# A projection computed with seven half products instead of eight, and its weight sums made partly by adding transfers

## The reference, cut to what matters

```
def swiglu(h, w_in, w_out):
    gu = h @ w_in
    gate, up = gu[..., :D_FF], gu[..., D_FF:]
    return (jax.nn.silu(gate) * up) @ w_out

        x = x + mla_attention(...)
        x = x + 0.5 * swiglu(rms_norm(x, g[2]), ffn_w_in[l, 1], ffn_w_out[l, 1])
return rms_norm(x, final_norm)
```

## Time and profile before

| what | value |
|---|---|
| time, median of 3 runs | 1777.91 us (1776.92 to 1777.92) |
| profiled execution, first to last instruction | 1777.1 us |
| PE busy | 1749.7 us (98%) |
| DVE / ACT / POOL busy | 931.8 / 651.0 / 322.9 us |
| traffic | 206.50 MB, mean 116 GB/s |

### The profile page before, as it was taken

One profiled execution on the slowest core, in us unless ns is written; L12 is line 12 of the kernel. 1 busy time (PEld: TensorE's weight loads), 2 busy tenths in 40 slices (PEclk: granted clock), 3 DMA queues, 4 the chain that ended last, 5 costly groups with the idle time before them and its releaser, 6 DMA issues.

```text
span 1777.1 us, 22440 instructions
## 1 busy us (share of the span) xinstructions
PE 1749.7 (98%) x8598; PEld 1432.7 (81%) x8598; DVE 931.8 (52%) x1066; ACT 651.0 (37%) x896; POOL 322.9 (18%) x276
## 2 busy tenths in 40 slices
PE   9999999997999999999999999999999999999998
PEld 6888887876888888888888888888777888888887
DVE  7778898648555334433374444333774544433333
ACT  6332333347334333322253333222574443333222
POOL 8997273015013000000100000000200200000000
PEclk9999999999999999999999999999999999999999
DMA  5464556698333333323323332333310333323321
GB/s 192 128 171 132 172 149 167 205 319 274 119 95 96 99 101 94 94 95 96 94 83 112 101 94 94 95 96 100 101 36 8 121 97 94 94 94 96 102 86 48
DMA packets 80788, 206.50 MB, mean 116 GB/s; under 512 B 24048, under 2 KB 34416, under 8 KB 79696
## 3 DMA queue, kind: packets, MB, share of 16 engines
q1 hardware_dynamic: 69664, 189.86, 34.2%
q0 software_dynamic: 2592, 13.51, 2.3%
q10 hardware_dynamic: 8464, 2.20, 0.5%
HBM read 182.46 MB, written 23.07 MB: 116 GB/s over the span
## 4 chain that ended last, share of the span: by engine, by line
PE 85%; DVE 6%; ACT 3%; DMA 2%; issue 2%; SPq 1%; ACTq 0%; DVEq 0%
PE bank L1642 27%; PE bank L1644 27%; PE bank L1643 27%; DVE w_split L1183 2%; PE bank L2002 1%; ACT w_split L766 1%; DMA op_slot<-s_ops 1%; DVE g_split L1197 1%; PE bank L1981 1%; DMA s_y<-u_and_y 1%; ACT x_gained L797 0%; ACTq L799 0%; DMA s_ops<-ops_out 0%; DMA x_res<-xT 0%; SPq L448 0%
## 5 line engine op out<-in xcount | busy, mean ns | idle before, releaser
L1183 DVE TENSOR_TENSOR w_split<-w_raw,w_split 128x1024 fp32r<-128x1024 f32 x296 | 404.2, 1370 | 607.3 <-ACT w_split L766 606.3
L1642 PE MATMUL bank<-h_split,w_split 128*128 128x512 f32 x1504 | 589.9, 392 | 5.7 <-DVE gate L1195 2.5
L1644 PE MATMUL bank<-h_split,w_split 128*128 128x512 f32 x1504 | 585.9, 390 | 0.0
L1643 PE MATMUL bank<-h_split,w_split 128*128 128x512 f32 x1504 | 585.9, 390 | 0.0
L766 ACT ACTIVATE w_split<-w_raw 128x1024 fp32r<-128x1024 f32 x296 | 311.9, 1058 | 606.3 <-PE bank L1644 598.0
L1642 PEld LDWEIGHTS bank<-h_split,w_split 128*128 128x128 f32 x1504 | 282.6, 188 | 69.3 <-DVE gate L1195 4.6
L1643 PEld LDWEIGHTS bank<-h_split,w_split 128*128 128x128 f32 x1504 | 282.8, 188 | 59.3 <-issue 1.2
L1644 PEld LDWEIGHTS bank<-h_split,w_split 128*128 128x128 f32 x1504 | 282.7, 188 | 59.2
L1642 PE MATMUL bank<-g_split,w_split 128*128 128x512 f32 (+1 forms) x854 | 328.3, 384 | 0.4 <-DVE g_split L1416 0.4
L1644 PE MATMUL bank<-g_split,w_split 128*128 128x512 f32 (+1 forms) x854 | 327.6, 384 | 0.0
L1643 PE MATMUL bank<-g_split,w_split 128*128 128x512 f32 (+1 forms) x854 | 327.6, 384 | 0.0
(11 more groups left out here) (298 smaller groups left out, 1148.0 us busy)
## 6 DMA issues: line engine op xcount, KB each, us to landing
w_raw<-wstream SPq DMA_DIRECT2D x296, 512.0 KB, 3.5
op_slot<-s_ops SPq DMA_DIRECT2D x5, 2048.0 KB, 12.0
s_ops<-ops_out SPq DMA_DIRECT2D x16, 512.0 KB, 3.1
op_slot<-s_ops POOLq DMA_DIRECT2D x3, 2048.0 KB, 14.1
s_ops<-c_pow POOLq DMA_DIRECT2D x8, 512.0 KB, 4.8
s_ops<-k_window SPq DMA_DIRECT2D x64, 64.0 KB, 3.4
x_res<-xT SPq DMA_DIRECT2D x8, 256.0 KB, 7.1
s_u<-x_gained ACTq DMA_DIRECT2D x8, 256.0 KB, 10.1
```

What stands on the lines that cost most here:

```text
L1183: tt(W[:, r, 1, :], RAW[:, r, :], W[:, r, 0, :].bitcast(F32), ALU.subtract).then_inc(s_lo, 1)
L1642: mm(bank, hi, x_hi, start=start, stop=True, skip_group_check=True)
L1643: mm(bank, hi, x_lo, start=False, stop=True, skip_group_check=True)
L1644: return mm(bank, lo, x_hi, start=False, stop=True, skip_group_check=True)
```

## The change

For the last feed-forward the 512 tokens are taken as two halves and the 8 input tiles as even and odd ones. A pair of a gate and an up tile is then a 2 x 2 block product, and it is computed with seven products of half the size and sums, in place of eight (pair 0 keeps the old form). A product is 4 blocks x 3 matmuls of 256 tokens: 84 matmuls a pair, for 21 pairs. The products need four sums of weight blocks (S1 to S4) and four sums of input tiles (T1 to T4). S1 and S3 are made by a transfer that GpSimd issues and that adds into the loaded block; S2 and S4 are made by GpSimd additions. DVE and ACT join the products in PSUM. The feed-forward is cut in two parts of 11 inner tiles: pairs 0 to 10, then all 8 output tiles over these, then pairs 11 to 21 and the output tiles again. Weights lie in 14 slots of 128 x 512 (in place of four packs of 1024), with loads, splits and products in a hand-written order. Some semaphores of earlier stages are merged; their waits stay where they were.

```diff
+SEVEN = {1: (A11, B11), 2: (A12, B21), 3: (S4, B22), 4: (A22, T4), 5: (S1, T1), 6: (S2, T2), 7: (S3, T3)}
+SLOTS = 14
+SPLITS = {1: (A12, 2), 2: (S1, 2), 3: (S4, 1), 4: (S3, 2)}
...
 SP
+            sp.wait_ge(s_used, WO + 5)
+            load_sum1(1)
...
+                    sp.wait_ge(s_prod, DONE[5, u - 2])
+                    load_sum1(u)
+                    sp.wait_ge(s_prod, DONE[2, u - 2])
+                    load_first(u)
+                    if u > first:
+                        sp.wait_ge(s_prod, DONE[4, u - 3])
+                        load_sum3(u - 1)
...
 GpSimd
+            def add_sum1(u):
+                pool.wait_ge(s_ld[unit_slot(u, S1)], LOADED[u, S1])
+                pool.dma_start(raw(u, S1), wunit[u - 1][:, 0:512], accum_op=ALU.add).then_inc(s_sum1, 16)
...
+            def sum2(u):
+                pool.wait_ge(s_ld[unit_slot(u, A12)], LOADED[u, A12])
+                pool.wait_ge(s_sum1, 16 * u)
+                tt(raw(u, S2), raw(u, S1), raw(u, A11), ALU.add).then_inc(s_sums, 1)
+            def sum4(u):
+                pool.wait_ge(s_sums, 2 * u - 1)
+                tt(raw(u, S4), raw(u, S2), raw(u, A12), ALU.add).then_inc(s_sums, 1)
+            def unit_sums(u):
+                add_sum1(u)
+                pool.wait_ge(s_prod, DONE[6, u - 2])
+                sum2(u)
+                pool.wait_ge(s_prod, DONE[3, u - 2])
+                sum4(u)
+            for k in range(1, 6):
+                square_sum(N_IN1B, k)
+            add_sum1(1)
+            sum2(1)
+            pool.wait_ge(s_used, WO + 6)
+            sum4(1)
...
+            for u in range(3, 11):
+                unit_sums(u)
+                add_sum3(u - 1)
...
 ACT
+            unit_hi(1, 2)
+            act.wait_ge(s_kv_read, DT - 1 + 4)
+            product_input(4)
+            product_input(5)
+            act.wait_ge(s_used, WO + DT)
+            product_input(6)
+            act.wait_ge(s_x, X_BASE[WO] + DT)
+            product_input(7)
...
+            for u in range(2, 10):
+                unit_hi(u + 1, 1)
+                copy_fifth(u)
+                copy_first(u)
+                silu(u - 1)
+                unit_hi(u + 1, 2)
+                unit_hi(u + 1, 3)
+                unit_hi(u, 4)
+                copy_first_and_sixth(u)
+                unit_g_hi(u - 1)
...
 DVE
+            slots_lo(1, 1)
+            slots_lo(1, 2)
+            product_lo(4)
+            product_lo(5)
+            add_wo(DT - 1)
+            product_lo(6)
+            product_lo(7)
+            t_sums(2)
+            t_sums(3)
+            slots_lo(1, 3)
+            t_lo(2)
+            t_lo(3)
+            mean_rcp(N_IN1B, BK[6])
+            slots_lo(2, 1)
+            slots_lo(2, 2)
+            gate_scale(0)
+            slots_lo(2, 3)
+            slots_lo(1, 4)
+            gate_up(0)
+            for u in range(2, 10):
+                gate_sum(u - 1)
+                unit_g_lo(u - 2)
+                gate_scale(u - 1)
+                slots_lo(u + 1, 1)
+                up_second(u - 1)
+                slots_lo(u + 1, 2)
+                slots_lo(u + 1, 3)
+                slots_lo(u, 4)
+                gate_up(u - 1)
...
 PE
+            def unit(u, first):
+                if u >= 3:
+                    pe.wait_ge(s_read, F_BASE[FFN1B] + u - 2)
+                unit_product(5, u)
+                unit_product(1, u)
+                if u > first:
+                    pe.wait_ge(s_snap, snap(u - 1, 2))
+                    unit_product(7, u - 1)
+                pe.wait_ge(s_snap, snap(u, 0))
+                unit_product(2, u)
+                pe.wait_ge(s_snap, snap(u, 1))
+                unit_product(6, u)
+                if u > first:
+                    pe.wait_ge(s_up, u - 1)
+                    unit_product(4, u - 1)
+                unit_product(3, u)
...
+            stat(N_IN1B, BK[6])
+            pe.wait_ge(s_t_lo, 4)
+            for u in range(1, 11):
+                unit(u, 1)
+            for d in range(DT):
+                out_tiles_of(0, d)
+            for u in range(11, 22):
+                if u in (11, 12):
+                    pe.wait_ge(s_x, X_AT[0] + (6 if u == 11 else 8))
+                unit(u, 11)
+            for d in range(DT - 1):
+                out_tiles_of(1, d)
...
-                    if q == 1 and f == 8:
+                    if q == 1 and f == 5:
                         half_stat(0)
-                    if q == 1 and f == 14:
+                    if q == 1 and f == 9:
                         half_rstd(0)
```

More of the change, by code:

```diff
@@ new lines, with unit_slot, products_of @@
+PAIR_SLOTS = (10, 12)
+H_PLACE = (2, 3, 0, 1)
+def unit_slot(u, a):
+    return (0 if u % 2 else 7) + a
+def products_of(u):
+    part = PARTS[u // HALF]
+    before = u - 1 >= part[0] and u - 1 > 0
+    return ([(5, u), (1, u)] + [(7, u - 1)] * before + [(2, u), (6, u)] + [(4, u - 1)] * before + [(3, u)])
+PROD = []
+for part, units in enumerate(PARTS):
+    for u in units:
+        PROD += products_of(u) if u else [("pair", 0), ("pair", 1)]
+    PROD += [(7, units[-1]), (4, units[-1])] + [("out", part, o) for o in range(HALF if part == 0 else HALF - 2)]
@@ new lines, with split_at, load_slot @@
+STEP = {key: n + 1 for n, key in enumerate(SPLIT)}
+def split_at(key):
+    if key[0] == "pair":
+        return PAIR_SLOTS[key[1]], 2
+    if key[0] == "out":
+        return OUT_SLOTS[key[1]][key[2]], 2
+    first, n = SPLITS[key[1]]
+    return unit_slot(key[0], first), n
+LOADS = [("pair", 0), ("pair", 1)]
+for part, units in enumerate(PARTS):
+    LOADS += [(u, a) for u in units if u for a in (A12, S1, S3)]
+    LOADS += [("out", part, o) for o in range(HALF)]
+def load_slot(key):
+    return unit_slot(*key) if len(key) == 2 and key[0] != "pair" else split_at(key)[0]
@@ L101, with snap @@
+LOADED = {}
+for key in LOADS:
+    LOADED[key] = 16 * (1 + sum(load_slot(k) == load_slot(key) for k in LOADED))
+def snap(u, n):
+    return 3 * (u - 1) + n + 1
 G_IN0A, G_S5, G_IN0B, G_KV, G_IN1A, G_DQ, G_IN1B, G_FIN = (8 * i for i in range(8))
@@ L749, in _ @@
+            add_sum3(21)
+            for k in range(1, DT - 1):
+                square_sum(N_FINAL, k)
         @block.scalar
@@ L1123, in _ @@
                     square(N_IN1B, d - 1)
[L1125 to L1133, removed]
+                    product_input(d - 1)
+                if d == 4:
+                    t_hi(0)
@@ new lines, in _ @@
+            product_input(6)
+            act.wait_ge(s_x, X_BASE[WO] + DT)
+            product_input(7)
+            square(N_IN1B, 7)
+            unit_hi(1, 3)
+            t_hi(2)
+            t_hi(3)
+            copy_fifth(1)
+            copy_first(1)
+            unit_hi(2, 1)
+            unit_hi(2, 2)
+            root(N_IN1B)
+            nc.scalar.preload_act_table(ACT.Silu)
+            silu(0)
+            unit_hi(2, 3)
+            unit_hi(1, 4)
+            copy_first_and_sixth(1)
@@ L1592, in _ @@
                     add_wo(d - 1)
-            for k in range(DT):
-                if k == 4:
-                    add_wo(DT - 1)
-                h_lo(k, G_IN1B, H, H_BASE[FFN1B])
-            ffn_in(FFN1B, N_IN1B)
-            ffn_out(FFN1B, last=False)
+                if 1 <= d <= 4:
+                    product_lo(d - 1)
+                if d == 2:
+                    t_sums(0)
+                if d == 4:
+                    t_sums(1)
+                    t_lo(0)
+                if d == 6:
+                    t_lo(1)
+                    slots_lo("pair", 0)
+                    slots_lo("pair", 1)
```

491 lines of the change are left out of this document (442 added, 49 removed).

## The result

The kernel after takes 1805.62 us (median of 4, 1800.8 to 1806.8), the kernel before 1777.41 us beside it (4 runs, 1776.7 to 1777.9): ratio 1.0154, interval 1.0140 to 1.0168. It is 28 us slower; the forecast was 6.5 us faster, and 1805.6 lies above the range. The profiled execution took 1805.54 us, 2.0 us more than its span.

The account below looks back on a forecast made before the run. TensorE's matmul issue was taken as the bound (busy 98%). Projection -17.0, output -0.4, start +9.6, tail +1.3 gave -6.5 us: 1777.9 to 1771.4 us, range 1763 to 1786.

Parts of the forecast that it names:

- Matmul rate, projection and output: TensorE, last feed-forward: narrow matmuls 0.1199 us apart; projection saves 17.0 us over 21 pairs, output 0.4.
- Rival 4: TensorE: narrow matmuls don't keep 0.12 us between so many waits; at 0.1295 the total is 1788 us; chance 0.04.
- The adding transfer: GpSimd's adds into S1 and S3: 5 us from issue to landing, bounds 2.6 to 9.8, steady pairs free.
- Rival 1: Adding transfer slow, at unit_hi(u, 4) on ACT and S2 on GpSimd: 1793 us at L = 7.5; chance 0.18.
- L = 6.4: L is an adding transfer's time from issue to landing; at 6.4 us the steady ring is tight, then about 1 us per pair.
- The ring: Steady pairs' critical ring of waits, through S3's add and ACT's list: 2.4 us to spare at L = 5.
- The start: Stage's first pairs: 6.2 us lost waiting for t_lo behind the first add, 3.4 in pair 2; 9.6 in all.
- I leave it alone: TensorE's clock: at its upper level, 2.4 GHz, granted 1.00, throughout, so no term was given to it.
- Output and seams: Output tiles and the seam between the two parts: nothing waits at the seam, extra DVE additions lie under matmuls.
- The tail: Last output tile: add_half(1) waits for DVE behind final(0, 0..4); 1.3 us lost, between 0.2 and 1.7.
- Rival 2: Start covered: first add lands in 2.6 to 3 us, loss there 2 to 5 us, total 1765; chance 0.16.
- Rival 3: VectorE becomes the bound: GpSimd and DVE block each other fully, up to 0.4 us a pair, total 1779; chance 0.10.

Follow-up runs that it names:

- reorder: Kernel after with split (u, 4) moved behind other ScalarE and VectorE work, so S3's add no longer holds that work: 1812.84 us, ratio 1.0203.
- warm: Kernel after with S1's first add issued two square sums earlier and filler matmuls in two TensorE waits of the start: 1800.04 us, ratio 1.0126.
- no_adds: Kernel after with both adding transfers left out, S1 and S3 unsummed (result not the reference's): 1777.58 us, ratio 1.0003.
- swap: Kernel after with S3's add put between GpSimd's sums for S2 and S4, apart from S1's add: 1795.55 us, ratio 1.0108.
- one_add_warm_table: Kernel after with one adding transfer per pair, earlier first add, start fillers, and pair 2's splits ahead of the table loads: 1787.69 us, ratio 1.0056.
- its two relatives: Same one-add kernel with earlier first add and no fillers, without and with pair 2's splits ahead of the table loads: 1786.05 and 1783.35 us.

## Why the prediction was wrong

**Matmul rate, projection and output: right.** 0.1200 us against 0.1199, and free pairs took exactly 80.6 and 90.7 us. The gain of 17.4 us was real. Rival 4 falls.

**The adding transfer: the step that failed.** "I take 5, the row of equal size and queue", and with it a steady pair that waits for nothing. S1's add took 6.5 us in the median and 7.4 in the mean where the ring is closed, and the steady pairs lost 18.9 us. The bounds, 2.6 to 9.8, held it; the value taken did not. The nearest row was of a transfer that only copies. Rival 1 named the mechanism, the place (S2 on GpSimd) and the point from which it decides, L = 6.4, and by its rule 7.4 costs 17 x (7.4 - 6.4) = 17 us in the steady pairs, near the 18.9. Its total at 7.5, 1793, was still 12.6 us short, because the start and the seams were mis-sized as well (below). Its chance of 0.18 was too small for a cost without any row of its kind.

**The ring: half right.** The forecast ran it through S3's add and ACT's list, 2.4 us to spare, and said that S1's "comes out of cover at L = 5.3". The trace shows a shorter one, S1's add alone with GpSimd's 3.7 us of sums, issue and hand-overs: 7.0 + 3.7 = 10.7 in the turn shown. It needs no ACT, and in `reorder`, where ACT's list no longer stands behind S3's add, it keeps its length. It too is tight at 10.07 - 3.7 = 6.4, so the number agreed by luck.

**The start: 9.6 forecast, 18.8 measured.** The first part was near: add at 1402.0 forecast and 1401.0 measured, landed 1407.0 and 1406.7, sum4 done 1409.6 and 1409.5; that these agree is partly luck, since the add started 1.0 us earlier and took 5.7 us, not 5. Then VectorE's work took 15.3 us, not 13.0: the splits and the low parts run beside GpSimd's square sum and its sums for pair 2 (3.34 and 3.42 us for two, instead of 2.4). I had allowed 0.5 to 1 us for this in the steady pair and nothing in the start. A further 3.0 is that the stage began earlier here while VectorE's chain did not. In pairs 1 and 2 I had 3.4, and 7.1 were lost: the exposed table loads were in the forecast; the lower clock after the waits was not ("I leave it alone"); in `warm`, without it, the pairs gained 1.2 us and the total nothing.

**Output and seams: nothing forecast, 7.0 lost.** "At the seam between the parts nothing waits." In no_adds 2.8 of the 7.0 remain (1.3 + 1.5), so the rest comes with the adds; I have not separated it further.

**The tail: 1.3 forecast, 1.9 measured**, by the steps given: the addition of half 1 stood behind the five final operations, and TensorE's wait for the last square grew from 0.6 to 1.9 us.

**Rival 2** (the start is covered) fails: the first add took 5.7 us and the start lost 18.8. **Rival 3** (VectorE the bound) fails for the steady pairs: VectorE is busy 18.1 of 30 us there, and no_adds runs them free. In the start it is what remains.

The misses add up: steady 18.9 + start 9.2 + seams 7.0 + tail 0.6 - 3.0 (earlier stages) = 32.7, and 1770.6 (the forecast's span) + 32.7 = 1803.3.

Open: why an add beside another needs 7 us when alone it needs 4.8, since in swap a distance of 1.8 us helped in the second part and not at the end of the first; why the second part of one_add_warm_table was 7 to 8 us longer than in its two relatives; and how much of the adds' cost is taken by slower loads of the other queue (5.3 against 3.7 us). A kernel with the adds on another engine's queue was not tried.

## What to carry to other kernels

Before a sum is handed to an adding transfer, look for a row of one: a copy of equal size and queue says too little (3.8 against 4.8 alone and 6.5 in company). Where one engine issues such a transfer, stands for it and then works, add up that engine's own turn and compare it with the period, before any longer chain. And an edit that saves TensorE 0.8 us a pair has to pay for its start: here 12 to 15 us of exposed work at the stage's beginning ate most of a gain of 17, even with the adds at no cost.

## What the runs showed of the hardware

- An adding transfer of 256 KB took 4.0 (S3's) and 4.8 us (S1's) alone, in the median, and 5.0 and 6.5 as one of two per pair (8.5 at most); a copy took 3.4 and 3.8. The instruction that issues it lasted 0.85 to 1.17 us, a copy's 0.54.
- With two adds per pair the loads of 512 KB on SyncE's queue landed in 5.3 us (166 to 175 GB/s in steady windows), beside two plain copies in 4.4 (180 GB/s), without either in 3.7 (126 to 134 GB/s).
- After a wait of 3.1 us narrow matmuls came 0.213 us apart for 5.4 us (granted clock 0.50), then 0.120 (granted 1.00). Removing this with matmuls in the wait left the total unchanged.
